# Router products in column groups, and the work around the routing put in another order, in a one-core transformer kernel

## The reference

```
logit_g = (xt @ w_group + b_group)                  # 512 tokens, 4 groups
g_sel = argmax(logit_g);  gate_g = softmax(logit_g)[g_sel]
logit_e = (xt @ w_router + b_router)[group g_sel]   # 4 experts of the group
top_v, top_i = top_k(softmax(logit_e), 2);  top_v /= sum(top_v)
y = sum over the two experts of  top_v * gate_g * ((silu(x @ w_gate[e]) * (x @ w_up[e])) @ w_down[e])
```

## Time and profile before

| | |
|---|---|
| median of 3 runs | 891.4 us (891.25 to 894.61) |
| the profiled execution | 891.35 us, span 889.6 us |
| PE busy | 876.1 us (98%) |
| DVE busy | 463.6 us (52%) |
| ACT busy | 207.8 us (23%) |
| POOL busy | 181.3 us (20%) |

### The profile page before, as it was taken

The page is one execution under the profiler, slowest core; times in us unless marked ns, Lnnn a source line. Parts: engine busy times, 40 slices in busy tenths (PEclk is TensorE's granted clock), DMA queues, the critical chain, the costliest instruction groups (busy, mean ns, idle before and its releaser), DMA issues.

```text
span 889.6 us, 13643 instructions
## 1 busy us (share of the span) xinstructions
PE 876.1 (98%) x5554; PEld 500.4 (56%) x5554; DVE 463.6 (52%) x1014; ACT 207.8 (23%) x457; POOL 181.3 (20%) x164
## 2 busy tenths in 40 slices
PE   8999999999999989999999999999999999999998
PEld 5588875455665543333333333344688888866653
DVE  2764542457673356640941923548635542354756
ACT  2211213345554220010010010014201111543330
POOL 3212221000002036041041010033201303096000
PEclk9999999999999999999999999999999999999999
DMA  9945549224010749999999999971382101610002
GB/s 327 335 114 190 190 157 387 96 95 190 1 48 0 282 156 338 386 420 421 424 424 421 426 425 428 404 272 48 111 159 94 62 24 59 212 62 1 1 1 95
DMA packets 54831, 184.30 MB, mean 207 GB/s; under 512 B 15048, under 2 KB 15716, under 8 KB 48496
## 3 DMA queue, kind: packets, MB, share of 16 engines
q1 hardware_dynamic: 46368, 162.41, 48.6%
q0 software_dynamic: 4912, 14.18, 4.4%
q10 hardware_dynamic: 3488, 6.82, 2.0%
HBM read 168.70 MB, written 16.79 MB: 209 GB/s over the span
## 4 chain that ended last, share of the span: by engine, by line
PE 86%; DVE 4%; DMA 3%; POOL 2%; issue 2%; ACT 2%; SPq 0%; POOLq 0%; DVEq 0%; ACTq 0%
PE psum L1012 21%; PE psum L1216 16%; PE psum L1231 9%; PE psum L1114 6%; PE psum L916 5%; PE psum L1062 4%; PE psum L1039 4%; PE psum L1483 3%; PE psum L1368 2%; PE psum L1321 2%; PE psum L1076 2%; PE psum L1093 2%; PE psum L1430 2%; PE psum L1464 1%; PE psum L975 1%
## 5 line engine op out<-in xcount | busy, mean ns | idle before, releaser
L1216 PE MATMUL psum<-ring,buf_a 128*32 128x512 f32 x1296 | 165.9, 592 | 1.5 <-issue 1.5
L1216 PEld LDWEIGHTS psum<-ring,buf_a 128*32 128x32 f32 x1296 | 50.5, 110 | 95.4 <-issue 93.5
L2804 POOL DMA_INDIRECT buf_b<-xq_d,o_sb x48 | 53.2, 1109 | 159.3 <-DVE buf_a L2330 126.9
L2358 DVE TENSOR_TENSOR pT<-buf_d,psum 32x128 f32<-32x128 f32 x128 | 49.5, 387 | 67.6 <-PE psum L1216 65.9
L1231 PE MATMUL psum<-ring,s_buf 128*32 128x512 f32 x672 | 83.4, 592 | 0.0
L2735 POOL TENSOR_TENSOR qk_st<-qk_st,half 128x8 f32<-128x8 f32 x26 | 43.6, 1678 | 160.2 <-DVE qk_st L2424 74.4
L1012 PE MATMUL psum<-ring,buf_a 128*128 128x256 f32 x320 | 70.9, 380 | 0.0
L1978 DVE TENSOR_TENSOR s_buf<-s_buf,psum 128x512 f32<-128x512 f32 x52 | 35.3, 685 | 61.2 <-PE psum L1012 58.7
L1012 PE MATMUL psum<-ring,buf_b 128*128 128x256 f32 x288 | 64.8, 380 | 0.0
L1012 PEld LDWEIGHTS psum<-ring,buf_a 128*128 128x128 f32 x320 | 60.1, 190 | 8.2 <-issue 0.4
L1012 PEld LDWEIGHTS psum<-ring,buf_b 128*128 128x128 f32 x288 | 53.9, 190 | 7.5 <-issue 0.6
(11 more groups left out here) (336 smaller groups left out, 1324.1 us busy)
## 6 DMA issues: line engine op xcount, KB each, us to landing
ring<-in_moe_w_up SPq DMA_DIRECT2D x14, 2048.0 KB, 17.2
ring<-in_moe_w_down SPq DMA_DIRECT2D x14, 2048.0 KB, 16.6
ring<-in_moe_w_gate SPq DMA_DIRECT2D x13, 2048.0 KB, 14.5
ring<-in_w_in SPq DMA_DIRECT2D x7, 2048.0 KB, 14.7
ring<-in_w_ada SPq DMA_DIRECT2D x6, 2048.0 KB, 9.4
ring<-in_da_w_in SPq DMA_DIRECT2D x5, 2048.0 KB, 15.9
buf_c<-in_moe_w_gate SPq DMA_DIRECT2D x3, 2048.0 KB, 13.4
y_d<-ring POOLq DMA_DIRECT2D x1, 5632.0 KB, 22.1
```

The lines of the kernel that those rows point to most:

```text
L1216: last = mm(buf("mm", n)[rows, :], x_part[:, j, k, :], moe_weights(moe_load(q, m, r), KD)[:, k, :], start=(k == 0), stop=(k == KD - 1))
L2358: last = V.tensor_tensor(hid[s % 2][SUB * to:SUB * (to + 1), j * P:(j + 1) * P].rearrange("p (k a) -> p k a", k=FC), sg[s % 3][rows, colum ...
L2804: pool.indirect_dma_start(out=xg[:, s % 2, j * 256:(j + 1) * 256], out_offset=None, in_=xn_quarters, in_offset=bass.IndirectOffsetOnAxis(a ...
```

## The change

The matrix `w_rt` is padded with zeros from 20 to 32 columns, and the product of piece k goes to the 32 PSUM rows of group k % 4. So four groups hold partial sums; ACT copies all 128 rows, and the turn of the logits becomes a product with `four_sum`, a 128 x 20 matrix of ones and zeros that adds the four groups. `picks` moves into the space of `w_rt`.

In PE's program the two context transposes and two and a half of the 16 context products move ahead of the routing of the last tile, the others are divided anew around `places` and `ids`, and `last_T` moves from behind the first down to just ahead of the first gate. ACT's copies move with them. DVE makes the operand of `last_T` (`last_picks`) right behind `idx`, not behind `spill_places`.

```
-    w_rt = sb("w_rt", [P, KD, 20])
+    w_rt = sb("w_rt", [P, KD, 32])
+    four_sum = sb("four_sum", [P, 20])
...
-        def router_three(lo, hi):
-
-            for k in range(lo, hi):
-                drained(pe, "tp", turn["tp", "xT2", k])
-                mm(buf("mm", n_r)[0:20, 0:LAST], w_rt[:, k, :], xT2[:, k, 0:LAST], start=(k == 0), stop=(k == KD - 1))
+        def router_product(k, lo, hi):
+
+            group = slice(32 * (k % 4), 32 * (k % 4 + 1))
+            return mm(buf("mm", n_r)[group, lo:hi], w_rt[:, k, :], xT2[:, k, lo:hi], start=(k < 4), stop=(k >= 4))
...
-        router_three(0, 6)
+        for k in range(KD):
+            drained(pe, "tp", turn["tp", "xT2", k])
+            router_product(k, 0, LAST)
+        cx_transposes(2)
+        cx_transposes(3)
+        cv_products(0, 2)
         pe.wait_ge(xs2_ready, TT)
...
-        router_three(6, KD)
+        cv_products(2, 3)
...
-            last = transpose(buf("mm", n)[:, t * 20:(t + 1) * 20], logit_T[:, t * P:(t + 1) * P], ident[0:20, 0:20])
+            last = mm(buf("mm", n)[:, t * 20:(t + 1) * 20], logit_T[:, t * P:(t + 1) * P], four_sum[:], start=True, stop=True)
         fill(last, "mm", n)
         gate_row(1)
-        cx_transposes(2)
-        cx_transposes(3)
-        cv_products(0, 3)
+        cv_products(3, 8)
...
-        cv_products(3, 7)
+        cv_products(8, 13)
...
-        cv_products(7, CT * KD)
+        cv_products(13, CT * KD)
+        n = turn["mm", "last_T"]
+        claim(pe, "mm", n)
+        for i in range(2 * TT):
+            c, t = i % 2, i // 2
+            pe.wait_ge(last_ready, i + 1)
+            last = mm(buf("mm", n)[:, t * P:(t + 1) * P], slot_pick[:, c * TT + t, :], ident[:],
+                      start=(c == 0), stop=(c == 1))
+        fill(last, "mm", n)
...
+        V.memset(w_rt[:, :, 20:32], 0.0).then_inc(w_rt_ready, 1)
+        V.tensor_reduce(four_sum[:], ident[:].rearrange("p (g c) -> p c g", g=4)[:, 0:20, :], AX.X, ALU.add).then_inc(w_rt_ready, 1)
...
+        last_picks()
+
         def spill_places():
...
                 spill_places()
-                last_picks()
```

More of the change, by code:

```diff
@@ L169, in moe_steps @@
         todo += [("up", b), ("up", c), ("down", a)]
-        if q == 0:
-            todo.append(("last_T", 0))
         todo.append(("down", b))
@@ L324, in build @@
     r_m = sb("r_m", [P, 6, TT])
-    picks = sb("picks", [P, 2, TT, EXPERTS])
+    picks = w_rt[:, 0:4, :].rearrange("p (c t) (h e) -> p c (t h) e", c=2, e=EXPERTS)
     sel_pad = sb("sel_pad", [P, 2 * TT + 1, EXPERTS])
@@ L357, in build @@
     sel = sel_pad[:, TT:2 * TT, :]
-    logit_T = pT[0:20, 0, :]
+    logit_T = pT[:, 0, :]
     last_pick = o_sb[:, 0:512]
@@ L493, in build @@
     book("sc", "cv")
+    for m in (2, 3):
+        book("tp", "cxT", m)
     for b in range(2):
         book("tp", "xT2_last", b)
-    for m in (2, 3):
-        book("tp", "cxT", m)
     book("mm", "router_T")
@@ L503, in build @@
     book("mm", "ids")
+    book("mm", "last_T")
     for name, m in moe_steps():
@@ L508, in build @@
             book("sc", "down", m)
-        elif name == "last_T":
-            book("mm", "last_T")
     for t in range(TT):
@@ L1144, in cv_products @@
                 fill(last, "sc", n)
-        pe.wait_ge(w_rt_ready, 1)
+        pe.wait_ge(w_rt_ready, 3)
         n_r = turn["mm", "router_T"]
         claim(pe, "mm", n_r)
-        def router_three(lo, hi):
-            for k in range(lo, hi):
-                drained(pe, "tp", turn["tp", "xT2", k])
-                mm(buf("mm", n_r)[0:20, 0:LAST], w_rt[:, k, :], xT2[:, k, 0:LAST], start=(k == 0), stop=(k == KD - 1))
+        def router_product(k, lo, hi):
+            group = slice(32 * (k % 4), 32 * (k % 4 + 1))
+            return mm(buf("mm", n_r)[group, lo:hi], w_rt[:, k, :], xT2[:, k, lo:hi], start=(k < 4), stop=(k >= 4))
         def gate_row(c):
@@ L1166, in _ @@
             transposes(n, [xs2_rows(TT - 1, k) for k in range(4 * b, 4 * b + 4)])
-        router_three(6, KD)
+        cv_products(2, 3)
         for k in range(KD):
             drained(pe, "tp", turn["tp", "xT2_last", k // 4])
-            last = mm(buf("mm", n_r)[0:20, LAST:SEQ], w_rt[:, k, :], xT2[:, k, LAST:SEQ], start=(k == 0), stop=(k == KD - 1))
+            last = router_product(k, LAST, SEQ)
         fill(last, "mm", n_r)
@@ L1242, in _ @@
                 down(s)
[L1243 to L1251, removed]
         spills = spill_count(pe)
@@ L1662, in _ @@
         norm2_squares(TT - 1)
+        cx_copies(2)
+        cx_copies(3)
         n = turn["tp", "xT2_last", 0]
@@ L1667, in _ @@
         filled(act, "mm", n)
-        drain(S.copy(logit_T, buf("mm", n)[0:20, :]), "mm", n)
+        drain(S.copy(logit_T, buf("mm", n)), "mm", n)
         def gate_row_copy(c):
@@ L1680, in _ @@
         gate_row_copy(1)
-        cx_copies(2)
-        cx_copies(3)
         n = turn["sc", "cv"]
@@ L1685, in _ @@
         drain(S.copy(cv_kept, buf("sc", n)), "sc", n)
+        n = turn["mm", "last_T"]
+        filled(act, "mm", n)
+        drain(S.copy(last_pick, buf("mm", n)), "mm", n)
         def y_copy(s):
@@ L1711, in _ @@
                 y_copy(s)
[L1712 to L1715, removed]
         spills = spill_count(act)
@@ L2101, in _ @@
         link(V.tensor_scalar(quarter[:], quarter[:], 4.0 * NO_ROW, None, ALU.add))
-        V.tensor_tensor(w_rt[:], w_rt[:], gain2[:].unsqueeze(2).to_broadcast([P, KD, 20]), ALU.mult).then_inc(w_rt_ready, 1)
+        V.memset(w_rt[:, :, 20:32], 0.0).then_inc(w_rt_ready, 1)
+        V.tensor_reduce(four_sum[:], ident[:].rearrange("p (g c) -> p c g", g=4)[:, 0:20, :], AX.X, ALU.add).then_inc(w_rt_ready, 1)
+        V.tensor_tensor(w_rt[:, :, 0:20], w_rt[:, :, 0:20], gain2[:].unsqueeze(2).to_broadcast([P, KD, 20]),
+                        ALU.mult).then_inc(w_rt_ready, 1)
         dve.wait_ge(lam_exp, 1)
@@ L2271, in _, with last_picks @@
               "mm", n)
+        def last_picks():
+            link(V.tensor_scalar(slot_f[:], at_row, -1.0, float((SETS - 1) * P), ALU.mult, ALU.add))
+            for i in range(2 * TT):
+                c, t = i % 2, i // 2
+                j = c * TT + t
+                V.tensor_scalar(slot_pick[:, j, :], slots_iota, slot_f[:, j:j + 1], weight[:, c, t:t + 1],
+                                ALU.is_equal, ALU.mult).then_inc(last_ready, 1)
+        last_picks()
         def spill_places():
@@ L2302, in spill_places @@
             V.tensor_copy(row_i[:], row_f[:]).then_inc(rows_ready, 1)
[L2304 to L2311, removed]
         def x_turn(s):
```

## The result

The change makes the kernel slower: 897.11 us (median of 8 runs, 896.49 to 898.86) against 891.5 us; the ratio is 1.0058 [1.0046, 1.0069]. The forecast was 894.2 us; the time lies 0.3 us above the upper end of its range. The profiled execution of the changed kernel took 897.14 us, span 895.4 us, which is 5.79 us more than that of before (the medians differ by 5.6), so the trace can stand for the timing.

The account below looks back on a forecast made before the run. The prediction took the order of PE's work (busy 98%) to bound the kernel. It summed 891.35 + 3.4 - 2.0 - 0.3 + 1.7 = 894.15, say 894.2 us, no change within 0.5%, range 888.8 to 896.8.

Parts of the forecast that it names:

- Router, logits, `idx`: Routing of the last tile: router products take 1.3 and 0.5 us, logits come 1.2 us earlier, `idx` 0.4 us earlier.
- The load to slot 1 and the gathers: Ahead of the first gate: the load, issued 5.6 us earlier, makes set 0's gathers land late; gate start +3.4 us.
- The rival in which gathers and load share the engines: Set 0 lands as before after POOL's gathers, first gate at 331.4; 889.0 to 890.7 us, chance 0.22.
- The clock: First gate: after PE's wait it starts at 1.2 GHz for 3.5 us, costing +1.7 us (bounds 0 and twice that).
- The hole at 352.88: PE's 0.30 us hole from DVE taking set 2 late: it goes as the first gate starts later, -0.3 us.
- `last_T`, -2.0 us: Its 16 records leave quad 0 and are free in PE's wait ahead of the first gate: -2.0 us.
- the products overlap: Denies the rival that grouped router products run at the ungrouped pace, chain 5.3 us later: 899.5 us, chance 0.04.
- it didn't stay low: Denies the rival that PE stays at 1.2 GHz through first gate and up, losing 7 us: 899.5 us, chance 0.10.

Follow-up runs that it names:

- Holding the load: The changed kernel with the load to ring slot 1 issued only once set 0's four gathers have landed; 892.79 us, ratio 1.001.
- run kept warm: The changed kernel with 36 products of ones behind `last_T`, to keep PE busy in its wait for set 0; 895.81 us, ratio 1.0047.
- Quarter packets: The changed kernel with the load to slot 1 issued as four quarter loads, with packets of 4 KB instead of 16; 895.58 us, ratio 1.0044.
- half a load less: The changed kernel with one 2 MB gate matrix load of quad 2 cut to its first half; 894.55 us, ratio 1.0031.
- run with groups, kept warm: The kernel before with column groups and sums alone, plus nine products of ones ahead of the last tile's transposes; 890.94 us, ratio 0.9986.

## Why the prediction was too low

*Router, logits, `idx`:* right. 1.50 and 0.64 us where 1.3 and 0.5 were taken; logits at 309.08 (309.1), `idx` at 322.10 (322.1).

*The load to slot 1 and the gathers:* right in mechanism. The load goes out at 324.74 (324.6), set 0's last piece is turned at 334.33, and the first gate starts at 335.52 (335.2): +3.75 where 3.4 was taken. Holding the load took it back. The rival in which gathers and load share the engines, so that set 0 lands as before, is out.

*The clock:* right in mechanism, too small. From the first gate's start to the issue behind it 9.70 us, where before it is 7.13 from 331.77 to the row at 338.90: +2.57, where 1.7 was taken and 3.4 was the bound. The clock stayed at half for about 5.2 us of the gate (0.52 in the window 335 to 341), not for the 3.5 of the execution's start. Those 3.5 were read from the pace of the records alone; the granted clock of the windows there (0 to 5 us) reads 1.00. The run kept warm shows that the loss was the clock's.

*The hole at 352.88:* gone, -0.5 with what passes overlap, where -0.3 was taken (the two issues at 345.22 and 365.82 are 20.60 apart, before 21.12).

***`last_T`, -2.0 us: the step that failed.*** The 2.0 us did leave quad 0, as the issue at 393.29 shows, and came back as waits of 0.65 and 1.24 us for weights, so the term was 0 at the end. The prediction took PE's 98% as proof that PE's order decides everywhere, and read the DMA share only around the routing. Windows of the kernel before from 400 us on would have shown 1.01: behind the pair of loads the stream needs 180.5 to 180.9 us, as much as PE's own work took (180.65).

With this the sum closes: 891.35 + 3.75 + 2.57 - 0.5 + 0 = 897.17 us against 897.14. Of the 3 us that the forecast was short, 2.0 are this step, 0.9 the clock and 0.35 the gate, less 0.2 at the hole.

*The other rivals:* the products overlap (0.64 us for 16 records); the clock came back within the first gate, so it didn't stay low.

The Trainium skill's rule of the prediction (DMA: Bandwidth & Descriptors, Queues, rings and completion order), by which an engine takes turns between its queues packet by packet, had spoken for gathers that keep moving. Quarter packets moved the first gate by 1.1 us of the 4.4 by which the load delays it, so the runs bear out a small part of it at most.

Open stays what holds a gather back beside a load in flight, and why the timed runs kept only 1.0 of the 2.6 us in the run kept warm. That the share of 1.01 is all of the stream's limit was not measured by itself; that half a load less moves the end was.

## What to carry to other kernels

An engine that is busy 98% of the time need not be the only bound of a stage: read the DMA share by stage as well. Where it was full here, a saving on PE behind the start of that stream came back as a wait for weights, while one ahead of it counted. When work is moved, follow what it releases: here the end of the context products released a 2 MB load into the gathers. And the holes of 9.0, 4.9 and 2.2 us on TensorE cost the slow clock behind them too; filling the first and the last with products of ones took that cost away in the traces, while in the timed runs the intervals with and without them overlap.

## What was not expected of the hardware

The granted clock fell after a hole of 2.21 us (mean 0.63 in the window 304 to 308, about 1 us after work had begun again at 303.94), while the hole of 1.50 us ahead of the first gate in the run with groups, kept warm, left it at 1.00.

A gather that POOL began 0.4 us ahead of a 2 MB load was held back by it: its piece was taken 4.8 us after POOL began (325.19 to 330.01), where one ahead of the load needed 2.9 (323.86 to 326.71).
